# The low part of every weight unit made on GpSimd instead of VectorE, in a float32 two-block model kernel

## The reference

```python
# first block, for each of 2 layers
h = rms_norm(x, norm_g[l])
... = jnp.split(h @ w_in[l], IN_OFFSETS, axis=-1)        # 11 parts of 512 columns, and 16 small ones
y_a = gmlp_branch(...)                                   # gelu, layer norm, a product over tokens
y_b = retention_branch(...)                              # rotary, masked attention, norm
y_c = gdn_branch(...)                                    # conv, chunks of 64, triangular solve, a scan
gates = jax.nn.sigmoid(jnp.einsum("bsd,dne->bsne", h, w_gate[l]))
x = x + jnp.sum(gates * proj, axis=2) @ w_out[l]
# second block: swiglu (width 2816), a mixer, swiglu, in 2 layers
h = (jax.nn.silu(gate) * up) @ w_out ;  x = x + 0.5 * rms_norm_2(h, g[1])
x = x + rms_norm_2(hybrid_mixer or recurrent_mixer(rms_norm_2(x, g[2])), g[3])
```

## Time and profile before

| | |
|---|---|
| median of 3 runs | 1969.39 us (1969.28 to 1971.48) |
| span of the profiled execution, first to last instruction | 1968.4 us |
| TensorE busy | 1799.5 us (91%) |
| VectorE busy | 1154.7 us (59%), of it 608.6 us line 1383 |
| ScalarE busy | 875.8 us (44%) |
| GpSimd busy | 11.4 us (1%) |

### The profile page before, as it was taken

How to read it: one execution, slowest core, us unless ns; L and a number is a source line. 1 busy time by engine, 2 the same in 40 slices (tenths; PEclk the granted TensorE clock), 3 DMA queues, 4 the chain that set the end, 5 groups by cost and what they waited for, 6 DMA issues and landing times.

```text
span 1968.4 us, 24530 instructions
## 1 busy us (share of the span) xinstructions
PE 1799.5 (91%) x10424; PEld 1486.3 (76%) x10424; DVE 1154.7 (59%) x1578; ACT 875.8 (44%) x1017; POOL 11.4 (1%) x24
## 2 busy tenths in 40 slices
PE   7899899898999988999898989899989998769996
PEld 5777788687877876888686757788868886558885
DVE  4776885556778656545556534554555455774554
ACT  5443444346244434444445633444444444644442
POOL 0000000000000000000000000000000000000000
PEclk9899999888999998999899968899999998879998
DMA  6231445432123644555442212555545554234552
GB/s 253 84 108 66 145 154 192 160 129 86 67 102 129 226 152 150 187 187 192 161 171 99 94 43 94 184 186 192 192 164 191 190 193 160 94 131 171 174 189 86
DMA packets 41438, 291.75 MB, mean 148 GB/s; under 512 B 4609, under 2 KB 4737, under 8 KB 7153
## 3 DMA queue, kind: packets, MB, share of 16 engines
q1 hardware_dynamic: 38720, 280.16, 39.9%
q0 software_dynamic: 2608, 10.03, 1.4%
HBM read 289.12 MB, written 1.05 MB: 147 GB/s over the span
## 4 chain that ended last, share of the span: by engine, by line
PE 75%; DVE 16%; ACT 5%; issue 3%; POOL 0%; DVEq 0%; ACTq 0%
PE pg L436 22%; PE pg L437 21%; PE pg L438 21%; DVE wl L1383 4%; PE ps L634 3%; PE ps L516 2%; ACT wh L993 2%; DVE x L1841 1%; PE ps L889 1%; PE ps L887 1%; DVE arena L1504 1%; DVE arena L1507 1%; PE ps L674 0%; DVE arena L1999 0%; DVE sm L1460 0%
## 5 line engine op out<-in xcount | busy, mean ns | idle before, releaser
L1383 DVE TENSOR_TENSOR wl<-raw,wh 128x2048 fp32r<-128x2048 f32 x266 | 608.6, 2292 | 518.6 <-ACT wh L993 517.6
L436 PE MATMUL pg<-wh,hTh 128*128 128x512 f32 (+1 forms) x2160 | 852.4, 395 | 43.6 <-DVE hTl L1424 11.3
L437 PE MATMUL pg<-wl,hTh 128*128 128x512 f32 (+1 forms) x2160 | 836.9, 387 | 0.0
L438 PE MATMUL pg<-wh,hTl 128*128 128x512 f32 (+1 forms) x2160 | 835.9, 387 | 0.0
L993 ACT ACTIVATE wh<-raw 128x2048 fp32r<-128x2048 f32 x266 | 508.9, 1914 | 525.6 <-PE pg L438 516.7
L436 PEld LDWEIGHTS pg<-wh,hTh 128*128 128x128 f32 x2160 | 412.8, 191 | 138.6 <-issue 46.3
L438 PEld LDWEIGHTS pg<-wh,hTl 128*128 128x128 f32 x2160 | 411.6, 191 | 83.1
L437 PEld LDWEIGHTS pg<-wl,hTh 128*128 128x128 f32 x2160 | 412.3, 191 | 76.7
L1072 ACT ACTIVATE arena<-pg,sm 128x512 f32<-128x512 f32 (+1 forms) x49 | 33.0, 673 | 163.4 <-PE pg L438 163.4
L516 PE MATMUL ps<-cst,x 128*128 128x128 f32 x128 | 27.6, 402 | 50.7 <-DVE x L1841 34.1
L516 PEld LDWEIGHTS ps<-cst,x 128*128 128x128 f32 x128 | 24.6, 215 | 53.6 <-DVE x L1841 36.2
(11 more groups left out here) (320 smaller groups left out, 1168.9 us busy)
## 6 DMA issues: line engine op xcount, KB each, us to landing
raw<-weights SPq DMA_DIRECT2D x266, 1024.0 KB, 4.8
arena<-wide POOLq DMA_DIRECT2D x9, 512.0 KB, 3.5
x<-x_in SPq DMA_DIRECT2D x1, 1024.0 KB, 5.0
cst<-const_tables POOLq DMA_DIRECT2D x1, 1024.0 KB, 5.1
plainh<-dist_tables POOLq DMA_DIRECT2D x2, 512.0 KB, 4.8
arena<-gate_mix POOLq DMA_DIRECT2D x1, 1024.0 KB, 5.8
y_out<-x POOLq DMA_DIRECT2D x1, 1024.0 KB, 4.5
arena<-token_mix POOLq DMA_DIRECT2D x2, 256.0 KB, 3.8
```

What stands on the lines that cost most here:

```text
L436: pe.matmul(dst, lh, rh, start=first, stop=False)
L437: pe.matmul(dst, lh, rl, start=False, stop=False)
L438: return pe.matmul(dst, ll, rh, start=False, stop=last)
L1383: tt(wl[:, slot, :], raw[:, u % RAW_SLOTS, :], wh[:, slot, :], ALU.subtract)\
```

## The change

The subtraction of all 266 units moves from DVE's program to GpSimd's. `POOL_UNITS` names the units that GpSimd makes (here all of them), `low_of(u)` gives the counter and the value that say "unit u's low part is there", and PE and SP wait on that. GpSimd's program is now a plain loop over the units that waits for ACT's copy only; its call does not stand between other work. GpSimd's side loads, the parameters, gains, tables and the store of the result are issued by ACT, at places in ACT's own program where the buffer that they write is free.

```diff
+LAYER_UNITS, FF_UNITS, HYB_UNITS, REC_UNITS = 44, 34, 30, 12
+POOL_UNITS = frozenset(range(LAYER_UNITS * DEPTH + 4 * FF_UNITS + HYB_UNITS + REC_UNITS))
+def low_of(u):
+    by_pool = len([v for v in POOL_UNITS if v <= u])
+    return ("low_pool", by_pool) if u in POOL_UNITS else ("low_dve", u + 1 - by_pool)
...
-                        pe.wait_ge(sem["split_low"], st.used + 1)
+                        low, count = low_of(st.used)
+                        pe.wait_ge(sem[low], count)
...
# ACT, in merge_out
+                if l == DEPTH - 1:
+                    act.dma_start(V(13824), wide[6]).then_inc(sem["final_g_landed"], 16)
                 gemm(D, (512,), ("evac_act",), read_gates(1, 1))
+                act.wait_ge(sem["params_used"], l + 1)
+                act.dma_start(par[:, :], params[l + 1]).then_inc(sem["params_landed"], 16)
...
# ACT, at the end
+            c.wait("x_ready", 2)
+            act.dma_start(out.rearrange("a (m p) d -> p (a m) d", p=P), x[:, :, :]).then_inc(sem["out_landed"], 16)
...
# DVE, pump
-                    dve.wait_ge(sem["split_high"], u + 1)
-                    tt(wl[:, slot, :], raw[:, u % RAW_SLOTS, :], wh[:, slot, :], ALU.subtract)\
-                        .then_inc(sem["split_low"], 1)
+                    if u not in POOL_UNITS:
+                        dve.wait_ge(sem["split_high"], u + 1)
+                        tt(wl[:, slot, :], raw[:, u % RAW_SLOTS, :], wh[:, slot, :], ALU.subtract)\
+                            .then_inc(sem["low_dve"], 1)
...
# SP
-                    sp.wait_ge(sem["split_low"], u - RAW_SLOTS + 1)
+                    low, count = low_of(u - RAW_SLOTS)
+                    sp.wait_ge(sem[low], count)
...
# GpSimd
+            for u in sorted(POOL_UNITS):
+                slot = u % SPLIT_SLOTS
+                pool.wait_ge(sem["split_high"], u + 1)
+                pool.tensor_tensor(wl[:, slot, :], raw[:, u % RAW_SLOTS, :], wh[:, slot, :], ALU.subtract)\
+                    .then_inc(sem["low_pool"], 1)
```

More of the change, by code:

```diff
@@ L276, in program @@
             "rope_done", "row_done", "rs_ready", "rv_ready", "sc_masked", "sc_ready", "small_done",
-            "small_read", "small_w_high", "small_w_low", "split_high", "split_low", "sq_done", "sq_free",
+            "small_read", "small_w_high", "small_w_low", "split_high", "low_dve", "low_pool", "sq_done", "sq_free",
             "sq_ready", "ssd_decay", "ssd_done", "ssd_mask", "state_ready", "state_scaled", "sv_done",
@@ L1183, in retention, with merge_out @@
                 prepare(4)
-            def merge_out():
+            def merge_out(l):
                 def read_gates(n, first=0):
@@ L1226, in gemm_out, with ffn @@
                 pump(st.used + 3)
-            def ffn(name):
+            def ffn(name, post, last_of_block=False):
                 features_of_x(lambda k: name[:, k:k + 1], X_AT)
+                load_gain(post)
+                if last_of_block:
+                    act.dma_start(V(11776, 2048).rearrange("p (t n) -> p t n", t=2),
+                                  gate_mix.rearrange("t p n -> p t n")).then_inc(sem["mix_landed"], 16)
+                    act.wait_ge(sem["params_used"], DEPTH + 1)
+                    act.dma_start(par[:, :], params[3]).then_inc(sem["params_landed"], 16)
                 hid = V(0, 2 * FF).rearrange("p (m f) -> p m f", m=M)
@@ L1241, in hybrid @@
                 features_of_x(lambda k: spar("g2")[:, k:k + 1])
+                load_gain(1)
                 z = V(10240, 2048).rearrange("p (m f) -> p m f", m=M)
@@ L1315, in recurrent @@
                 features_of_x(lambda k: rp("g2")[:, k:k + 1])
+                load_gain(4)
                 def read(i, pair, w):
@@ L1351, in recurrent, with load_gain @@
                 gemm_out(D)
+            def load_gain(i):
+                act.dma_start(V(13824), wide[i]).then_inc(sem["wide_landed"], 16)
             for l in range(DEPTH):
@@ L1355, in _ @@
                 features_of_x(lambda k: fp("norm_g")[:, k:k + 1])
+                act.dma_start(DIST, dist).then_inc(sem["dist_landed"], 16)
                 small_w(16, fp("small_w"))
                 gdn()
+                act.dma_start(LN_GAINS, wide[7 + l]).then_inc(sem["wide_landed"], 16)
+                act.dma_start(TOKEN_MIX, token_mix[l]).then_inc(sem["mix_landed"], 16)
                 retention()
-                merge_out()
+                merge_out(l)
             act.wait_ge(sem["params_landed"], 16 * 2)
             small_w(24, spar("small_w"))
-            ffn(spar("g0"))
+            ffn(spar("g0"), 0)
             hybrid()
-            ffn(spar("g4"))
+            ffn(spar("g4"), 2, True)
             act.wait_ge(sem["params_landed"], 16 * 3)
-            ffn(rp("g0"))
+            ffn(rp("g0"), 3)
             recurrent()
-            ffn(rp("g4"))
+            ffn(rp("g4"), 5)
+            c.wait("x_ready", 2)
+            act.dma_start(out.rearrange("a (m p) d -> p (a m) d", p=P), x[:, :, :]).then_inc(sem["out_landed"], 16)
+            act.wait_ge(sem["out_landed"], 16)
         @block.vector
```

1 line of the change is left out of this document (removed).

## The result

The changed kernel takes 2074.9 us (median, 2071.99 to 2079.6) where the kernel before took 1970.4 us beside it: a ratio of 1.0531, 95% interval 1.0515 to 1.0546, so 104 us slower. The forecast was 2007 us, with a range up to 2067 us. The sign is as forecast, the size is not: the loss is 2.8 times the forecast one.

The account below looks back on a forecast made before the run. PE bounds the long products, DVE's own instructions the scans, norms and mixer ends. Removed work -60, start +2 and waits +96 gave +38: 1968.4 + 38 + 1.0 = 2007 us, range 1905 to 2067.

Parts of the forecast that it names:

- rival (a): DVE and GpSimd run side by side, so only the removal counts: -58, 1911 us; chance 0.25.
- (b): GpSimd subtracts as fast as DVE (2.3 us) and they exclude each other: -25, 1944 us; chance 0.09.
- (c): GpSimd takes over 5.38 us per unit and becomes the bound: +350, some 2320 us; chance 0.06.
- Term 1: Subtractions leaving DVE: 52 us of pieces on the chain, 7 of waiting in `pump`, 1 for the store: -60.
- the start's +2: At the kernel's start GpSimd's longer subtraction isn't hidden by PE's work: +2.3 us.
- only what is on the chain counts: Of 609 us of subtractions leaving DVE, only 35 pieces on the chain of waits count, 76 us.
- 11 us taken off for pieces next to another wait: Five pieces ending beside a wait due within a microsecond, plus the mixers' ends, give nothing back: 11 us off the 76.
- Line 1634 at 199.60 us: DVE's step, ready while DVE waits for ACT's copy and subtracts, starts some 3.5 us earlier; 7 us over two layers.
- Term 2: DVE instructions with two SBUF inputs wait for the end of GpSimd's 4.6 us subtraction: +96.
- the count of windows: Windows of 4.6 us behind ACT's 266 copies: 30 hold a two-input DVE step on the chain (90 us), 20 off it (47).
- three windows of 11.1 us less 6.7: At `gmlp_values`, waits cost 11.1 us, against which 6.7 us of removed subtractions go; the sum takes off 2 x 3.
- PE has four units ahead: At `gmlp_values`, PE has 21.5 us of units before the waiting product, so removal returns 1 us per layer, not 6.7.

Follow-up runs that it names:

- the first run: Only the side loads and the store move to ACT's queue, DVE keeps all 266 subtractions, against the kernel before: 1969.1 us, ratio 0.9991.
- the run with 64 columns: Changed kernel, but from the fourth unit on GpSimd subtracts only 64 of each unit's 2048 columns, DVE none: 1928.2 us, ratio 0.9786 to the kernel before.

## Why the prediction failed

**What was right.** DVE's steps on SBUF and GpSimd's subtraction exclude each other, and this decides the sign; rival (a), side by side, is out by any of the timelines. GpSimd takes 4.62 us in a products' stretch, 4.6 forecast, so rivals (b) and (c) are out. The products hide it, 26 units in 140 us. The loads cost nothing on ACT: the first run. Transposes behind the second swiglu: "some 12 us", and 12.33 came. The start costs 2.3 us: DVE's first step behind it, line 1490 of before, came at 59.00 and comes at 61.25. The Trainium skill's rule of SBUF — State Buffer (section Who interferes with whom), that of two such instructions the second blocks until the first is through, agrees with the ends of the waits (line 1486 at 1546.28, GpSimd at 1546.24).

**Term 1, the removed work: -60 forecast, with the start's +2 a -58; measured -34** (-43 where the low part comes at once). The step that failed is "only what is on the chain counts", with 11 us taken off for pieces next to another wait. The chain shows who was last, and not how soon the next wait ends behind it. In the scan PE takes products of the next units between its own steps, and at the place below the wait for PE takes back most of what DVE wins. DVE's timeline at one such place, before:

```profile
151.71 2.29 DVE L1383 TENSOR_TENSOR wl<-raw,wh 128x2048 fp32r<-128x2048 f32 x1
153.92 0.87 DVE L1475 TENSOR_SCALAR arena<-plainh,sm 128x512 f32<-128x512 f32 x2
...
158.16 0.69 DVE L1591 TENSOR_TENSOR arena<-arena,ps 128x512 f32<-128x512 f32 x1 [0.59 <-PE ps L634]
```

and in the run in which GpSimd only writes:

```profile
153.02 0.88 DVE L1510 TENSOR_SCALAR arena<-plainh,sm 128x512 f32<-128x512 f32 x2
...
158.99 0.69 DVE L1626 TENSOR_TENSOR arena<-arena,ps 128x512 f32<-128x512 f32 x1 [2.31 <-PE ps L647]
```

The subtraction is gone, its successor leads by 0.90 us where it trailed by 1.3 before, and DVE stands 1.72 us longer at the next wait for PE: 2.21 us won, 1.73 given back. The end of the first layer (line 1769) comes 8.3 us earlier in that run and the end of the second 20.5 us. Line 1634 at 199.60 us does as forecast (3.69 us won), and 1.48 of it is given back at line 1652.

**Term 2, the waits: +96 forecast, +138 measured.** The step that failed is the count of windows, laid over the old trace, together with the share of the waits that reaches the chain. It gave 137 us of waits in 50 windows and put 0.70 of them on the chain; the changed kernel has 184 us. The same rule applied again to the two traces (the first DVE instruction with two SBUF inputs within 4.6 us behind each copy) gives 51 windows and 144 us. By unit, 43 of these 51 do hold DVE up, with 118 us forecast and 141 measured. Eight, with 26 us, stay empty. Fifteen more units hold it up where the rule found nothing, with 42 us, of which the kernel's first two units have 9. So the places were mostly right, the waits there 23 us too short, and the units that came in weigh 16 us more than those that fell out. One reason shows in the timeline of DVE in the scan's preparation, first layer, after:

```profile
126.56 5.01 DVE L1614 TENSOR_TENSOR arena<-arena,cst 128x512 f32<-128x512 f32 x1
131.61 0.69 DVE L1611 TENSOR_TENSOR arena<-arena,cst 128x512 f32<-128x512 f32 x1
132.22 5.00 DVE L1612 TENSOR_TENSOR arena<-arena,cst 128x512 f32<-128x512 f32 x1
```

The chain of lines 1611 to 1614 waits for unit 13 (GpSimd from 126.33 to 131.02), goes on for 1.2 us, and meets unit 14 (from 131.80) close to its start. In the old trace the chain was over by then, and the window of unit 14 was counted as empty. A chain that has been held up once is still there when the next subtraction begins. Five units, 14, 28, 58, 72 and 145, hold up in this way a chain that the unit before had held up, and have 21 of the 42 us; against 14 and 58 stand units 15 and 59 behind them, which stay empty.

The sizes, as an estimate: 13 of the 184 us stand at the first three units, where they cost nothing (DVE is 2.25 us late behind them, as forecast for the start). The other 171 make 120 us by the forecast's share of 0.70, 24 more than 96. The remaining 18 mean that a wait weighs more on the chain than I assumed.

"Instructions with two SBUF inputs wait" also left out those with one, and 46 of the 184 us stand in copies and in steps with a constant, such as line 1486 above. The same section of the Trainium skill says that copies and tensor-with-constant steps can take the shared pair of ports too; I had used only its sentence on two inputs, and the rows bear out both. But little of the missing 42 us comes from there. 37 of the 46 us stand in windows that the rule had counted, and behind each of the 14 such steps that waited over 0.4 us a step with two inputs follows before the same subtraction ends (line 1492 stands 0.5 us behind line 1486) and would have waited for the same end. The one-input steps add only the work between the two, 7 us in all 14. The second swiglu's end shows it: 4.26 us of one-input wait, and PE's transposes as late as forecast.

Two more things are in the difference, and neither was isolated. One: `gmlp_values` was taken as three windows of 11.1 us less 6.7. The chain of waits there, first layer, after:

```profile
273.70 4.71 issue
...
280.61 4.08 DVE sm L1775
284.71 4.50 DVE sm L1486
...
291.08 4.36 DVE sm L1493
...
299.24 3.40 PE L769 MATMUL ps<-arena 128*128 128x128 f32 x16 [11.66 <-DVE arena L1783]
```

Four waits of some 16.5 us (the "issue" is line 1761's) instead of three with 11.1; the fourth, line 1493 at 291.08, was in no window. From ACT's copy at 252.1 us of before to the one at 290.0 the distance to the old trace grows from 19.3 to 30.9 us, and at the same place of the second layer from 53.1 to 66.5: 25 us in both layers. The prediction's text gives 11.1 - 6.7 = 4.4 per layer, 9 in both; its sum takes off 3 instead of 6.7, which leaves 14 for both after the 1 us per layer in term 1. So 11 to 16 of the missing 42 us are here. My argument that PE has four units ahead stood on PE's place in the old run: PE comes late too, but uses that lead up and then idles for 11.66 us. Two: PE's clock. Windows of 10 us of the changed kernel (us, busy and count of PE, PEld, DVE, ACT, POOL; granted clock as a share of 2.4 GHz; DMA):

```profile
230.00:240.00 10.00, 7.08 (x35) 5.71 (x33) 9.97 (x5) 4.38 (x5) 9.06 (x2) 0.98 0.28 105
240.00:250.00 10.00, 6.93 (x26) 5.90 (x27) 8.75 (x24) 3.00 (x3) 1.82 (x1) 0.66 0.29 105
...
290.00:300.00 10.00, 0.76 (x3) 0.77 (x4) 9.62 (x13) 0.82 (x1) 4.51 (x1) 0.59 0.59 210
300.00:310.00 10.00, 10.00 (x48) 8.67 (x47) 2.60 (x9) 1.78 (x1) 0.00 (x0) 0.90 0.00 0
```

PE idled for 5.99 us before 243 and for 11.66 before 299; the windows with these gaps and behind them are granted 0.66, 0.59 and 0.90, so part of their time is at 1.2 GHz, where the kernel before had 1.00 in each window from 200 to 310 us. The same 10424 matmuls are busy for 1819.2 us, and for 1790.5 in the run without reads: 29 us, of which the part on the chain lies in the +138 and can overlap with the shares above. My sum had no such term.

**The account.** -34 for -58 is +24, +138 for +96 is +42: 66 of the 68 us between 2007 and 2074.9. The split into these two rests on the one run in which GpSimd only writes. Within term 2 the estimates of 24 and 18 us, the 11 to 16 us at `gmlp_values` and the clock are views of the same 42 us and don't add up.

## To carry to other kernels

Before work goes to GpSimd, lay its whole length over each DVE instruction that works on SBUF alone, with two inputs, or as a copy or a step with a constant, and expect a chain of tiny steps to pay for all that GpSimd has queued, in however many pieces. Move the chain on by each wait before looking at the next window: it may still be there. Take a piece on the chain of waits as an upper bound of what its removal gives: look how long the next wait behind it already is. Move the few units whose work is on the chain and meets nothing (ten of 266 gave 16 us), and look at the trace again after each move, since the windows shift.

## What the hardware showed beyond that

The wait runs both ways. In the run with 64 columns, GpSimd's subtraction takes 0.32 us, but 1.75 us where DVE is in the middle of an instruction with two SBUF inputs. GpSimd's timeline and DVE's:

```profile
304.04 0.32 POOL L2128 TENSOR_TENSOR wl<-raw,wh 128x64 fp32r<-128x64 f32 x1 [5.12 <-ACT wh L1005]
309.48 1.75 POOL L2128 TENSOR_TENSOR wl<-raw,wh 128x64 fp32r<-128x64 f32 x1 [5.12 <-ACT wh L1005]
...
308.76 2.29 DVE L1822 TENSOR_TENSOR arena<-arena 128x2048 f32<-128x2048 f32 x1
```

And it depends on both partners: beside GpSimd's writes DVE's steps with two SBUF inputs keep their 0.16 us (line 1493 at 1417.14), while 46 short ones of a tensor with a constant, or copies, take 0.29 to 0.58 us instead of 0.17 (line 1489 at 1415.98); over that whole run the groups with one input got 17 us longer.
